# Two 64-row score products side by side, with sums and a root moved, in a two-block decoder kernel

## The chip, the cores and the metric

The kernel runs on one core of one Trainium2 chip. The metric is device time of one execution in microseconds (us), the median of the runs; lower is better. TensorE (PE) multiplies, VectorE (DVE), ScalarE (ACT) and GpSimd (POOL) do the rest, SyncE (SP) issues nearly all transfers.

## The reference

512 tokens of width 1024 in float32 pass through two decoder blocks. The change touches two parts of them. In the first block's first layer an indexer with 16 heads of 64 scores all keys; each token keeps its best 128 keys and attends to them:

```python
dots = jnp.einsum('bqhd,bsd->bqhs', qi, k_idx).astype(jnp.float32)
score = jnp.einsum('bqhs,bqh->bqs', jax.nn.relu(dots), wi.astype(jnp.float32))
score = jnp.where(causal[None], score, -jnp.inf)
_, idx = lax.top_k(score, topk)
```

Both layers of the first block also attend to a memory of 256 rows, with 4 heads of 64:

```python
s = jnp.einsum('bshd,bmhd->bhsm', q, k).astype(jnp.float32) * MEM_HEAD_DIM ** -0.5
p = jax.nn.softmax(s, axis=-1)
o = jnp.einsum('bhsm,bmhd->bshd', p, v.astype(jnp.float32)).astype(q_mem.dtype)
```

Everything else (projections, the attention to the chosen keys, gated feed-forward layers, a second block) stays as it is.

## The kernel before

All activations lie feature-major, 128 features by 512 tokens. Weights stream in as 334 chunks of eight 128x128 blocks. Of each chunk ScalarE makes a rounded high part (`split_hi`, into `w_hi`) and VectorE or GpSimd the rest (`split_lo`, into `w_lo`); each block is then three products of TensorE in one pass (high x high, high x low, low x high), 24 products a chunk, in `project`. `raw`, `w_hi` and `w_lo` have two halves, so a chunk can be loaded only when the chunk two before it has been split, and split only when that one has been used (`chunk_used`). `pj` (two PSUM banks) takes the projections; `take` on ScalarE copies one out.

Each engine runs one program written out by hand, in order; semaphores tie them. The stages of the first layer that matter here are:

- **Front** (to about 56 us): chunk 0 (index key), then 32 small products that sum squares (`sums("amix")`), chunk 1, in the middle of it `spread("amix")`, which turns the root of the mean square into a row factor; chunk 2 (first two index heads); a turn of the index weights; chunk 3 block by block with `sums("mem")`. VectorE needs the factor for the tables of the rotation (`tables_by_factor`, then `rope`), and splits chunk 3 after that.
- **Index** (to 130 us): eight tiles of two heads. A tile has six units, (head, token block) for blocks 1 to 3, of width 256, 384 and 512. `kidx` holds the keys twice: in one copy the features of the second head are zero, in the other those of the first, so that a product over all 128 rows gives one head. A unit is one plain float32 product into `ps[u % 2]` on TensorE, a relu into `s_sb[u % 2]` on ScalarE (which counts up `score_taken`), and a multiply-add into `score` on VectorE (`idx_added`). Between units TensorE projects the query of tile t+2, and ScalarE takes it after the relu of unit 4.
- **Selection** (to 212 us): VectorE finds 8 keys at a time for three token blocks, 16 rounds of six instructions (`rounds(n)`). Meanwhile TensorE projects the latent (`ckv`, 2 chunks), sums its squares, projects the memory keys and values (8 chunks of 256 columns, `mem_k`, `mem_v`; GpSimd splits these chunks) and the first queries. Between its rounds VectorE works off `means("ckv")`, waits for GpSimd's `inverse_root("ckv")`, and later does `apply("ckv")`: two products `hf`, ScalarE's rounding `norm_hi("ckv")` (`c_hi`, written after the last of the eight memory chunks in ScalarE's program), two differences `c_lo`.
- **Attention** `aq`, then `amem` over the memory. `amem` and, in the second layer, `bmem` run 2 tiles of 8 units (head, block). A unit passes from TensorE (`score_`) to VectorE (`maximum`, L1303 and L1314), ScalarE (`softmax`, L757), TensorE (`turn_p`, L2022), ScalarE (`bring`, L770) and TensorE (`values`, L2062). TensorE's program at unit u is: score of u + `ahead` (3), turn of u+1, values of u. `mem_k` holds keys with zero halves, as `kidx`.

## Time and profile before

| | us |
|---|---|
| median of 3 runs (lowest, highest) | 2417.23 (2413.25, 2422.09) |
| the profiled run's own time | 2415.6 |
| its span in the trace | 2413.8 |
| TensorE busy | 2273.4 (94%) |
| VectorE busy | 1298.2 (54%) |
| ScalarE busy | 921.1 (38%) |
| GpSimd busy | 250.7 (10%) |

The kernel is one long chain of stages, and TensorE is busy in nearly all of them, so what matters is which stretches are not set by it. The granted clock is TensorE's: 1.00 stands for 2.4 GHz and 0.50 for 1.2 GHz. A float32 product appears in the trace as two records, each with its own weight load; a product of rounded parts as one. The starts of neighbouring records give their true pace, since the ends are modelled and overlap.

### The profile page before, as it was taken

Reading aid. Unit: us, or ns where it says so; the run is one execution under the profiler, and the core shown is the slowest. Engines: PE = TensorE matmul, PEld = TensorE weight load, DVE = VectorE, ACT = ScalarE, POOL = GpSimd, SP = SyncE. Lnnn points to the kernel's source line nnn. Section 1 sums busy time; section 2 is a strip of 40 time slices with the busy share of each in tenths; the row PEclk is TensorE's granted clock in tenths of the full one; section 3 lists DMA queues with packets and bytes.
Section 4 is the critical chain, followed back from the end, with each engine's and each line's share of the span. In section 5 each row is a group of like instructions: output and inputs, shape, how many; then the busy total and the mean of one; then the engine's idle time right before and its main releaser. Section 6 shows DMA issues by size and latency. Waiting matters only on the chain.

```text
span 2413.8 us, 34422 instructions
## 1 busy us (share of the span) xinstructions
PE 2273.4 (94%) x10882; PEld 1855.7 (77%) x10882; DVE 1298.2 (54%) x2537; ACT 921.1 (38%) x1850; POOL 250.7 (10%) x143
## 2 busy tenths in 40 slices
PE   7986999999999799999999999999999689999997
PEld 6675777888888687788888888888887667777766
DVE  5876444666644566466664454555544643545443
ACT  4433453322322266432223332222223334555551
POOL 0042221000001111110000210000002000011112
PEclk8998999999999999999999999999999889999888
DMA  3121111332333110223232332222222312000001
GB/s 131 51 88 53 61 53 62 96 101 90 104 102 102 66 36 26 77 90 99 93 104 96 104 97 96 99 99 96 96 96 79 113 63 85 2 19 9 19 10 70
DMA packets 50053, 182.93 MB, mean 76 GB/s; under 512 B 5552, under 2 KB 5680, under 8 KB 49840
## 3 DMA queue, kind: packets, MB, share of 16 engines
q1 hardware_dynamic: 49824, 181.35, 22.9%
q8 instruction: 44, 0.72, 0.1%
q0 software_dynamic: 144, 0.52, 0.1%
q14 instruction: 41, 0.34, 0.0%
HBM read 179.76 MB, written 2.10 MB: 75 GB/s over the span
## 4 chain that ended last, share of the span: by engine, by line
PE 83%; DVE 7%; issue 4%; ACT 3%; POOL 1%; DMA 1%; DVEq 0%; ACTq 0%; POOLq 0%; SPq 0%
PE pj L1863 68%; PE ps L2006 4%; PE po L2062 4%; PE pt L2022 2%; ACT w_hi L670 1%; DMA raw<-in_wstream 1%; PE po L2047 1%; PE ps L2176 1%; DVE s_sb L1303 1%; PE pj L1973 1%; DVE rtmp L1248 1%; DVE w_lo L1118 1%; PE po L2071 1%; ACT p_sb L757 1%; DVE rtmp L1245 1%
## 5 line engine op out<-in xcount | busy, mean ns | idle before, releaser
L1863 PE MATMUL pj<-h_hi,w_hi 128*128 128x512 f32 x1736 | 706.9, 407 | 21.0 <-DVE w_lo L1118 15.6
L670 ACT ACTIVATE w_hi<-raw 128x1024 fp32r<-128x1024 f32 x334 | 353.7, 1059 | 865.6 <-PE pj L1863 848.8
L1863 PE MATMUL pj<-h_lo,w_hi 128*128 128x512 f32 x1736 | 683.8, 394 | 0.0
L1863 PE MATMUL pj<-h_hi,w_lo 128*128 128x512 f32 x1736 | 683.6, 394 | 0.0
L1118 DVE TENSOR_TENSOR w_lo<-raw,w_hi 128x1024 fp32r<-128x1024 f32 x288 | 390.4, 1356 | 392.2 <-ACT w_hi L670 391.9
L1863 PEld LDWEIGHTS pj<-h_hi,w_hi 128*128 128x128 f32 x1736 | 331.1, 191 | 90.1 <-issue 17.1
L1863 PEld LDWEIGHTS pj<-h_hi,w_lo 128*128 128x128 f32 x1736 | 330.5, 190 | 71.1
L1863 PEld LDWEIGHTS pj<-h_lo,w_hi 128*128 128x128 f32 x1736 | 331.5, 191 | 64.6 <-issue 1.4
L1863 PE MATMUL pj<-G_hi,w_hi 128*128 128x512 f32 x704 | 278.1, 395 | 3.1 <-DVE G_lo L1367 3.0
L1863 PE MATMUL pj<-G_lo,w_hi 128*128 128x512 f32 x704 | 276.0, 392 | 0.0
L1863 PE MATMUL pj<-G_hi,w_lo 128*128 128x512 f32 x704 | 275.9, 392 | 0.0
L1303 DVE CUSTOM_DVE_ANT_0 s_sb<-ps,cst 128x256 f32<-128x256 f32 (+4 forms) x264 | 102.1, 387 | 174.2 <-PE ps L2006 125.1
L757 ACT ACTIVATE p_sb<-s_sb,stats 128x256 f32<-128x256 f32 (+4 forms) x288 | 140.0, 486 | 125.1 <-DVE stats L1317 124.0
L579 POOL TENSOR_TENSOR w_lo<-raw,w_hi 128x1024 fp32r<-128x1024 f32 x46 | 109.8, 2387 | 545.6 <-ACT w_hi L670 545.6
L1863 PEld LDWEIGHTS pj<-G_hi,w_hi 128*128 128x128 f32 x704 | 133.6, 190 | 35.1 <-DVE G_lo L1367 3.8
L1863 PEld LDWEIGHTS pj<-G_hi,w_lo 128*128 128x128 f32 x704 | 133.4, 190 | 28.2
L2022 PE MATMUL pt<-cst,p_sb 128*128 128x128 f32 (+1 forms) x640 | 129.8, 285 | 26.7 <-ACT p_sb L757 25.8
L1863 PEld LDWEIGHTS pj<-G_lo,w_hi 128*128 128x128 f32 x704 | 133.6, 190 | 27.3
L2022 PEld LDWEIGHTS pt<-cst,p_sb 128*128 128x128 f32 (+1 forms) x640 | 86.3, 148 | 78.3 <-ACT p_sb L757 41.8
L770 ACT ACTIVATE pT<-pt 128x384 f32<-128x384 f32 (+3 forms) x320 | 119.2, 372 | 69.9 <-PE pt L2022 67.2
L553 POOL TENSOR_TENSOR ssum<-sq 128x512 f32<-128x512 f32 x6 | 9.4, 1563 | 981.1 <-ACT sq L837 981.1
L1170 DVE TENSOR_TENSOR fr<-pj,fac_f 128x512 f32<-128x512 f32 x44 | 30.4, 692 | 105.3 <-PE pj L1863 101.1
(295 smaller groups left out, 2531.4 us busy)
## 6 DMA issues: line engine op xcount, KB each, us to landing
raw<-in_wstream SPq DMA_DIRECT2D x334, 512.0 KB, 3.4
xT<-in_x SPq DMA_DIRECT2D x4, 512.0 KB, 9.5
out_x<-xT SPq DMA_DIRECT2D x4, 512.0 KB, 2.7
memT<-in_mem SPq DMA_DIRECT2D x1, 1024.0 KB, 12.3
cst<-in_cst SPq DMA_DIRECT2D x1, 512.0 KB, 10.5
tab<-in_tab POOLq DMA_DIRECT2D x1, 512.0 KB, 5.0
posi<-in_pos SPq DMA_DIRECT2D x1, 256.0 KB, 2.8
vec<-in_vec SPq DMA_DIRECT2D x1, 182.5 KB, 2.4
```

What stands on the lines that cost most here:

```text
L579: nc.gpsimd.tensor_tensor(w_lo[:, here], raw[:, here], w_hi[:, here].bitcast(f32), ALU.subtract).then_inc(lo_ready, 1)
L670: nc.scalar.activation(w_hi[:, c.par * CW:(c.par + 1) * CW], raw[:, c.par * CW:(c.par + 1) * CW], ACT.Copy).then_inc(hi_ready, 1)
L757: nc.scalar.activation(p_sb[:, par * S:par * S + w], s_sb[:, par * S:par * S + w], ACT.Exp, scale=rsm[:, b:b + 1] if branch == "mem" else ...
L770: nc.scalar.activation(pT[rows, par * S:par * S + n], pt[par][rows, 0:n], ACT.Copy).then_inc(pT_ready, 1)
L1118: nc.vector.tensor_tensor(w_lo[:, here], raw[:, here], w_hi[:, here].bitcast(f32), ALU.subtract).then_inc(lo_ready, 1)
L1170: nc.vector.tensor_tensor(dst, pj[t.par][:, 0:n], fac[name][:, 0:n], ALU.mult).then_inc(pj_free[t.par], 1)
L1245: link(nc.vector.stream_shuffle(rtmp[:, :], src, mask))
L1303: nc.vector.tensor_tensor_reduce(out=s_sb[:, par * S:par * S + w], in0=ps[par][:, 0:w], in1=bias(ph, u), scale=1.0, scalar=-3.0e38, op0=AL ...
L1863: mm = nc.tensor.matmul(acc, w[:, col:col + P], x[part], start=first and k == 0, stop=last and k == 2)
L2006: nc.tensor.matmul(ps[u % 2][:, 0:w], q[:, par * S + b * P:par * S + (b + 1) * P], keys, start=True, stop=True).then_inc(score_done, 1)
L2022: mm = nc.tensor.transpose(pt[par][0:wide, k * P:(k + 1) * P], p_sb[:, par * S + k * wide:par * S + (k + 1) * wide], ident)
L2062: mm = nc.tensor.matmul(acc, pT[:, par * S + k * P:par * S + (k + 1) * P], val, start=k == 0, stop=k == kbs - 1)
```

## The change

Keys are stored once, 64 rows for each head. The score of a head multiplies only its 64 rows, and the two heads of a block stand next to each other, so that the products use different halves of the array's rows. TensorE waits once for a pair, until both banks are free. `IDX_UNITS` and the memory units are ordered block by block; in `amem` and `bmem` TensorE issues the pair of u+2 and u+3 at each even u (`ahead` falls from 3 to 2). VectorE's add for the second head waits for the first head's. The blocks of the next index query follow each pair, three, three and two. In the front the squares are summed between the blocks of chunk 1, `spread("amix")` stands behind chunk 2, and the turn of the index weights behind chunk 3. In the selection `means("ckv")` follows 3 rounds instead of 6 and `apply("ckv")` 8 instead of 10, and GpSimd's root for it follows the third chunk instead of the sixth.

```diff
-        self.ahead = 3 if self.m == 8 else 2
+        self.paired = branches == ["mem"]
+        self.ahead = 3 if self.m == 8 and not self.paired else 2
...
-IDX_UNITS = [(hh, b) for hh in range(2) for b in range(1, NB)]
+IDX_UNITS = [(hh, b) for b in range(1, NB) for hh in range(2)]
...
+    beside = [(hh, b) for b in range(NB) for hh in range(2)]
...
-                if c == CH["mem"] + 5:
+                if c == CH["mem"] + 2:
                     inverse_root("ckv")
...
-            squares("amix", lambda m: (x_loaded[m // 2], 16))
             c, t = At(CH["afront"]), At(TL["afront"])
+            squares("amix", lambda m: (x_loaded[m // 2], 16), 0, 4)
             split_hi(c + 2)
             take(qn[:, 0:S], t, c)
+            squares("amix", lambda m: (x_loaded[m // 2], 16), 4)
             tables(0)
+            split_hi(c + 3)
             spread_factor("amix")
...
-            link(rope(ktmp[:, S:2 * S], qn[:, 0:S], tab_a, SHUF64, t))
-            for hh in range(2):
-                last = nc.vector.tensor_scalar(kidx[:, hh * S:(hh + 1) * S], ktmp[:, S:2 * S], V("half", hh), None,
-                                               ALU.mult)
-            last.then_inc(roped, 1)
+            rope(kidx[:, :], qn[:, 0:S], tab_a, SHUF64, t).then_inc(roped, 1)
...
-                    dve.wait_ge(idx_added, s + 1)
+                    dve.wait_ge(idx_added, s + 1 + hh)
...
-            rounds(6)
+            rounds(3)
             means("ckv")
             dve.wait_ge(rs_ready, STATS.index("ckv") + 1)
             nc.vector.tensor_tensor(rck[:, 0:NB], r4[:, 0:NB], rsa[:, 0:NB], ALU.mult).then_inc(rck_ready, 1)
+            rounds(5)
+            apply("ckv")
             rounds(4)
-            apply("ckv")
-            rounds(2)
...
-                pe.wait_ge(score_taken, ph.first_score + t * ph.n + u + 1)
-                nc.tensor.matmul(ps[u % 2][:, 0:w], q[:, par * S + b * P:par * S + (b + 1) * P], keys,
+                if not (ph.paired and hh):
+                    pe.wait_ge(score_taken, ph.first_score + t * ph.n + u + (2 if ph.paired else 1))
+                rows = slice(hh * 64, hh * 64 + 64) if branch == "mem" else slice(0, P)
+                nc.tensor.matmul(ps[u % 2][:, 0:w], q[rows, par * S + b * P:par * S + (b + 1) * P], keys[rows],
...
-                    score_(ph, i, j, u + ph.ahead)
+                    if not ph.paired:
+                        score_(ph, i, j, u + ph.ahead)
+                    elif u % 2 == 0:
+                        for e in range(2):
+                            score_(ph, i, j, u + 2 + e)
...
-            sums("amix")
-            pe.wait_ge(ld["cst"], 16)
-            for some in (range(4), range(4, CB)):
-                project(At(CH["afront"] + 1), At(TL["afront"] + 1), h_hi, h_lo, some=some)
-                if 0 in some:
-                    spread("amix")
+            for k in range(CB):
+                project(At(CH["afront"] + 1), At(TL["afront"] + 1), h_hi, h_lo, some=range(k, k + 1))
+                sums("amix", range(k, k + 1))
...
-                    if u < 4 and more:
-                        idx_query(i, j + 2, range(2 * u, 2 * u + 2))
+                    if hh and more:
+                        idx_query(i, j + 2, (range(0, 3), range(3, 6), range(6, CB))[u // 2])
             idx_query(0, 0)
-            turn(At(TL["afront"] + 1), TN["widx"])
+            pe.wait_ge(ld["cst"], 16)
+            spread("amix")
             for k in range(CB):
                 idx_query(0, 1, range(k, k + 1))
                 sums("mem", range(k, k + 1))
+            turn(At(TL["afront"] + 1), TN["widx"])
...
-                if k == 5:
+                if k == 4:
                     spread("ckv")
```

Left out above: `squares` and `take` get arguments for this, `mem_k` is written by one copy instead of two, the plain score of the index stage is cut into two 64-row halves in the same way, and the buffers shrink.

Three places show the order. The first is TensorE at the start of `amem`; `ps<-mem_k` is a score, `pt<-cst,p_sb` a turn (two products a unit), `po<-mem_v` the values (two a unit). Before:

```order
L2022 MATMUL pt<-cst,p_sb 128x128 [waits pT_ready,exp_done]
L2022 MATMUL pt<-cst,p_sb 128x128
L2062 MATMUL po<-mem_v_123,pT 128x64 [waits pT_ready,out_ready]
L2062 MATMUL po<-mem_v_123,pT 128x64
L2006 MATMUL ps<-mem_k_122,qn 128x256 [waits score_taken]
L2022 MATMUL pt<-cst,p_sb 128x128 [waits pT_ready,exp_done]
L2022 MATMUL pt<-cst,p_sb 128x128
L2062 MATMUL po<-mem_v_123,pT 128x64 [waits pT_ready]
```

And with the change, from the same turn (of unit 1) on, with its pair of scores ahead of it:

```order
L2002 MATMUL ps<-mem_k_122,qn 128x256 [waits score_taken]
L2002 MATMUL ps<-mem_k_122,qn 128x256
L2018 MATMUL pt<-cst,p_sb 128x128 [waits pT_ready,exp_done]
L2018 MATMUL pt<-cst,p_sb 128x128
L2058 MATMUL po<-mem_v_123,pT 128x64 [waits pT_ready,out_ready]
L2058 MATMUL po<-mem_v_123,pT 128x64
L2018 MATMUL pt<-cst,p_sb 128x128 [waits pT_ready,exp_done]
L2018 MATMUL pt<-cst,p_sb 128x128
L2058 MATMUL po<-mem_v_123,pT 128x64 [waits pT_ready]
L2058 MATMUL po<-mem_v_123,pT 128x64
L2002 MATMUL ps<-mem_k_122,qn 128x256 [waits score_taken]
L2002 MATMUL ps<-mem_k_122,qn 128x256
```

Before, a score stood ahead of every turn, of the unit two turns later; now two scores stand ahead of two turns, and the second of these turns is that of the first of the two scores.

The second place is TensorE at the end of an index tile (`pj<-h..` are products of the query of tile t+2, `ps<-kidx` scores). Before:

```order
L1863 MATMUL pj<-h_hi,w_hi 128x512
L1863 MATMUL pj<-h_lo,w_hi 128x512
L1863 MATMUL pj<-h_hi,w_lo 128x512
L2175 REGISTER_ALU
L2176 MATMUL ps<-kidx,qs 128x384 [waits score_taken]
L2175 REGISTER_ALU
L2176 MATMUL ps<-kidx,qs 128x512 [waits score_taken]
L2171 REGISTER_ALU
L2175 ISA [waits roped]
L2176 MATMUL ps<-kidx,qs 128x256 [waits score_taken]
```

With the change:

```order
L2175 MATMUL ps<-kidx,qs 128x512 [waits score_taken]
L2175 MATMUL ps<-kidx,qs 128x512
L1858 MATMUL pj<-h_hi,w_hi 128x512
L1858 MATMUL pj<-h_lo,w_hi 128x512
L1858 MATMUL pj<-h_hi,w_lo 128x512
L1858 MATMUL pj<-h_hi,w_hi 128x512
L1858 MATMUL pj<-h_lo,w_hi 128x512
L1858 MATMUL pj<-h_hi,w_lo 128x512
L2168 REGISTER_ALU
L2173 ISA [waits roped]
L2175 MATMUL ps<-kidx,qs 128x256 [waits score_taken]
L2175 MATMUL ps<-kidx,qs 128x256
```

The last two blocks of the query have moved behind the scores of units 4 and 5. The third place is ScalarE in the same tile, with the change; its order is that of before except for the widths (before: 384, the copy, 512, the split, 256):

```order
L937 ACTIVATE s_sb<-ps 128x512 [waits idx_added,score_done]
L926 REGISTER_ALU
L677 REGISTER_ALU [waits roped]
L678 ACTIVATE qn<-pj 128x512 [waits chunk_used]
L935 REGISTER_ALU
L937 ACTIVATE s_sb<-ps 128x512 [waits idx_added,score_done]
L670 ISA
L672 ACTIVATE w_hi<-raw 128x1024 [waits chunk_used,chunk_loaded0]
L935 ISA
L937 ACTIVATE s_sb<-ps 128x256 [waits idx_added,score_done]
```

The copy of the query (`qn<-pj`, which waits for the whole query) has stayed between the relus of units 4 and 5.

## Rows read from the trace of the kernel before

**Rows 1.** waits of TensorE: us in total, times, longest us

```profile
PE pt L2022 <- ACT p_sb L757: 25.8, 18, 16.1
```

**Rows 2.** timeline, VectorE, selection: start us, us, instruction [idle before <-releaser]

```profile
133.77 1.48 DVE L1620 MAX8 m<-score 128x8 f32<-128x256 f32 x3 [0.20 <-DVE score L1613]
...
167.34 0.16 DVE L1631 TENSOR_TENSOR rck<-r,rsa 128x4 f32<-128x4 f32 x1 [8.90 <-POOL r L567]
...
182.09 1.41 DVE L1227 SCALAR_TENSOR_TENSOR hf<-ckv,vec,po 128x512 f32<-128x512 f32 x2 [0.21 <-DVE score L1624]
...
185.95 1.48 DVE L1620 MAX8 m<-score 128x8 f32<-128x256 f32 x3 [0.27 <-DVE c_lo L1213]
```

**Rows 3.** timeline, same stage, on TensorE, GpSimd and ScalarE

```profile
146.25 0.99 PE L1907 MATMUL po<-ones,sq 128*128 128x1 f32 x4
...
152.93 2.40 POOL L579 TENSOR_TENSOR w_lo<-raw,w_hi 128x1024 fp32r<-128x1024 f32 x1 [7.88 <-ACT w_hi L670]
...
165.67 1.64 POOL L567 TENSOR_TENSOR r<-v,mhalf 128x8 f32<-128x8 f32 x1
...
183.21 0.63 ACT L979 ACTIVATE mem_v<-pt,rv 128x128 f32<-128x128 f32 x2 [4.91 <-PE pt L1949]
183.72 1.15 ACT L710 ACTIVATE c_hi<-hf 128x512 fp32r<-128x512 f32 x2
```

**Rows 4.** timeline, bmem attention: TensorE (4), VectorE (1), ScalarE (2)

```profile
964.07 0.44 PE L2022 MATMUL pt<-cst,p_sb 128*128 128x128 f32 x2 [0.28 <-ACT p_sb L757]
...
967.75 0.65 PE L2006 MATMUL ps<-mem_k,qn 128*128 128x256 f32 x2
...
968.24 0.38 PE L2022 MATMUL pt<-cst,p_sb 128*128 128x128 f32 x2
...
968.85 0.65 PE L2006 MATMUL ps<-mem_k,qn 128*128 128x256 f32 x2
...
968.62 0.42 DVE L1303 CUSTOM_DVE_ANT_0 s_sb<-ps,fac_mem 128x256 f32<-128x256 f32 x1 [0.42 <-PE ps L2006]
...
963.32 0.60 ACT L757 ACTIVATE p_sb<-s_sb,stats,rsm 128x256 f32<-128x256 f32 x1 [0.40 <-DVE stats L1314]
...
969.34 0.60 ACT L757 ACTIVATE p_sb<-s_sb,stats,rsm 128x256 f32<-128x256 f32 x1
```

**Rows 5.** timeline, index stage: TensorE (2), ScalarE (2)

```profile
66.10 0.58 PE L1863 MATMUL pj<-h_hi,w_hi 128*128 128x512 f32 x1
...
75.52 0.58 PE L1863 MATMUL pj<-h_hi,w_hi 128*128 128x512 f32 x1
...
65.59 0.59 ACT L676 ACTIVATE qn<-pj 128x512 f32<-128x512 f32 x1
...
66.55 1.06 ACT L670 ACTIVATE w_hi<-raw 128x1024 fp32r<-128x1024 f32 x1
```

**Rows 6.** chain in order of time (start us, us, what); timeline of ScalarE

```profile
130.56 10.91 PE pj L1863 x48
...
141.56 1.06 ACT L670 ACTIVATE w_hi<-raw 128x1024 fp32r<-128x1024 f32 x1 [3.89 <-PE pj L1863]
```

**Rows 7.** TensorE by shape: 32-row and 128-row products: xcount | busy, mean ns

```profile
L2047 PE MATMUL po<-cmp_v,pT 32*128 x64 | 15.0, 317 | 0.0
...
L2062 PE MATMUL po<-n_vs,pT 128*128 x160 | 21.7, 267 | 0.0
```

**Rows 8.** timeline of the front: TensorE, then VectorE

```profile
35.39 0.60 PE L1930 MATMUL po<-cst,r 128*128 128x128 f32 x4
...
46.30 0.38 PE L1907 MATMUL pt<-ones,sq 128*128 128x1 f32 x2 [0.98 <-ACT sq L685]
...
42.31 1.22 DVE L1118 TENSOR_TENSOR w_lo<-raw,w_hi 128x1024 fp32r<-128x1024 f32 x1
```

**Rows 9.** busy us by stretch (PE PEld DVE ACT POOL), granted clock, DMA

```profile
27.50:31.00 3.50, 3.50 (x18) 3.50 (x18) 1.23 (x1) 3.10 (x5) 0.00 (x0) 0.50 0.02 5
...
122.70:130.20 7.50, 6.75 (x15) 2.98 (x16) 5.93 (x12) 3.23 (x7) 0.00 (x0) 0.77 0.00 0
```

More of the change, by code:

```diff
@@ L676, in take, with squares @@
                 nc.scalar.activation(dst, pj[t.par][rows, 0:n], func, scale=scale).then_inc(pj_free[t.par], 1)
-            def squares(name, waits):
+            def squares(name, waits, start=0, stop=None):
                 src, n, _, _, _, _ = NORM[name]
-                for m in range(dict(NORMS)[name]):
+                for m in range(start, stop or dict(NORMS)[name]):
                     sem_, value = waits(m)
@@ L941, in _ @@
             idx_query(0, 0)
+            squares("mem", lambda m: (ld["mem"], 16))
             act.wait_ge(v_turned, TN["widx"] + 1)
@@ L944, in _ @@
                                  ACT.Copy, scale=1024.0 ** -0.5)
[L945 removed]
+            split_hi(At(CH["idx"] + 3))
             tables(1)
[L947 removed]
             idx_query(0, 1)
@@ L968, in _ @@
                     if k < 2:
-                        act.wait_ge(chunk_used, c.v + 3)
-                        for hh in range(2):
-                            last = nc.scalar.activation(mem_k[l][:, (2 * k + hh) * MEM:(2 * k + hh + 1) * MEM],
-                                                        pj[t.par][:, 0:MEM], ACT.Copy, scale=V("half", hh))
-                        last.then_inc(pj_free[t.par], 1)
+                        take(mem_k[l][:, k * MEM:(k + 1) * MEM], t, c, n=MEM)
                     else:
@@ L1995, in score_ @@
                 elif branch == "mem":
-                    k_at = (2 * t + hh) * MEM
-                    keys = mem_k[0 if ph.name == "amem" else 1][:, k_at:k_at + MEM]
+                    keys = mem_k[0 if ph.name == "amem" else 1][:, t * MEM:(t + 1) * MEM]
                 elif branch == "band":
```

22 lines of the change are left out of this document (10 added, 12 removed).

## The prediction

> **What bounds the kernel now.** I read the chain of work that ended last and TensorE's list of waits first. TensorE is busy for 94% of the span, so a stretch of the change is worth something only where TensorE sets its end, and the question of each stretch is what ends last there. TensorE's longest single wait, 16.1 us, is at the start of the attention `aq` [rows 1]: all of the selection stage is set by VectorE's 16 rounds, not by TensorE. The timeline of that stage shows VectorE's two waits, 8.90 us for GpSimd's root and the time from `hf` to the end of `c_lo` [rows 2], and what held the root and ScalarE's `c_hi` back [rows 3]. The timeline of `bmem` shows a ring of three engines, in which a unit's score, maximum, exponential, turn and values follow each other [rows 4]. In the index stage TensorE is the bound, with 9.42 us a tile [rows 5].
>
> **Selection, +7.3 us.** Four rounds fill 167.5 to 182.1 us, 3.65 us each [rows 2]. Before, `apply("ckv")` begins at 182.09, after 10 rounds, and ends at 185.7. Its second half needs `c_hi`, and ScalarE writes `c_hi` at 183.72, right behind the last `mem_v`, for which it had waited 4.91 us on TensorE [rows 3]: that time is TensorE's, which works through ckv, eight memory chunks and the first query. Nothing in the change shortens that list. With the change VectorE does 3 rounds to 144.7 us (10.9 us from 133.77). It then waits for the sums of squares, which end at 147.2 [rows 3]. The root follows GpSimd's third split, which ends at 155.3, and takes 1.64: 157.0, where before it came at 167.3. Five rounds end at 175.4, the two `hf` at 176.8, and there VectorE waits 7 us for the same `c_hi` at 183.7. `apply` ends at 185.7 as before, but with 8 rounds behind it instead of 10: two rounds more to do, 2 x 3.65 = 7.3 us. The earlier root earns nothing, since the wait has moved to `c_hi`. TensorE's 16.1 us wait grows by as much, so all of it is on the path. Bounds: 5.6 if TensorE's list ends 1.7 us sooner, because the root no longer stands between two later splits; 8.9 if the root, now ahead of the fourth split, delays it by its 1.64.
>
> **Memory attention, +11 us for both.** The steps of the ring from start to start are: score to maximum 0.87, maximum to exponential 0.72 (967.75, 968.62, 969.34), exponential to turn 0.75 (963.32, 964.07), turn through values to next score 0.61 (968.24, 968.85) [rows 4]. Before, a score stood two turns ahead of its own turn, and a unit came each 1.10 us (967.75, 968.85). With the change a pair of scores is followed by two turns, the second of which belongs to the first score of the pair; the next pair stands behind it. So one pair needs a whole ring: 0.87 + 0.72 + 0.75 + 0.61 = 2.95, with ScalarE's copy between turn and values 3.0 us, where two units took 2.2. That is +0.8 for each of the five full rounds of the ring in a stage of eight pairs (the ends of the stage balance): +4.0 a stage. What the narrower products save on TensorE is hidden here, since TensorE waits. On top comes the clock: with 1.3 us of products in 3.0 instead of in 2.2 TensorE is less busy, and where scores alone ran, at 122.7 to 130.2 us, the granted clock was 0.77 on the mean, a part of it at the level of 0.50 [rows 9]. At that level the product and the turn cost about 1.0 more in a ring. I take 1.5 a stage; the ends are 0 and 5. Sum (4.0 + 1.5) x 2 = 11, from 2 (if half of the ring is covered by something that I don't see) to 18.
>
> **Index stage, +5 us.** Of 9.42 us a tile [rows 5] the 24 products of a query take 24 x 0.227 = 5.45 (48 in 10.91 [rows 6]), so the six scores cost 3.97. Side by side they cost between 1.98 (the two heads fully together) and 3.97 (not at all). Each float32 product is two records in a row; of the four records of a pair only the second of the first head and the first of the second can lie side by side if records run in program order, as all timelines show them. I take three quarters, 2.98. The trace has no change between full and part-height products except the 32-row values of the compressed branch: 317 ns a record against 267 for 128 rows [rows 7]; 0.05 on four records gives 0.2 a pair, and 0 is the other end. I take 0.15, so 0.45 a tile. Then a new wait: the query's last two blocks now follow the scores of units 4 and 5, while ScalarE's copy of the query still stands between these two relus. TensorE ends the blocks, ScalarE starts 0.26 later (last product's pace end at 141.30, ScalarE at 141.56 [rows 6]), copy and relu take 0.96 (65.59 to 66.55 [rows 5]), the release 0.1: 1.3 us, in which TensorE waits for `score_taken` ahead of the next tile's pair. Queued behind it are that pair and all of the next query. Tile: 5.45 + 2.98 + 0.45 + 1.3 = 10.2, against 9.42: 6 x 0.8 = +4.7. VectorE (some 7.7 us a tile with its rotation, split and adds) fits inside, except in tiles 1 and 2, where the rotation of the latent key and a table come on top; the second head's relu now waits behind more of VectorE's list: +1.5. The last two tiles, without a query, gain 1. Together +5.2. The ends of the two unknown prices give tiles of 8.7 and 11.3: -4 and +12.
>
> A rule speaks for more. The Trainium skill, TensorEngine Tiling (Array Packing), Theoretical Speedup, gives up to 2 times where the contraction is 64 or less; with it and no other cost a tile would be 5.45 + 1.98 + 1.3 = 8.7. The same page, Key Properties, says that changing the tiling mode drains TensorE, which speaks against the change, as here it changes twice a pair. No row shows two products side by side.
>
> **Front, +1.5 us.** Eighteen records of the sums took 3.5 us at a granted clock of 0.50 [rows 9]; between dense blocks they should keep the full level, and with the blocks that followed at half speed this saves about 5 us. But the spread, at 35.39 before, now also stands behind four more blocks of chunk 1 and the eight of chunk 2, 12 x 0.68 = 8.2 us: 35.4 + 8.2 - 5 = 38.6. From the spread to the low part of chunk 3 VectorE needed 43.53 - 35.39 = 8.1 [rows 8], now 7.3 without the two products for the zero halves. Chunk 3 is ready at 45.9, and TensorE waits 7 us for it. Before, TensorE did its first block by 45.3, when a wait of 1.0 for the memory squares began [rows 8], so it had begun some 0.9 earlier, at 44.4: chunk 3 starts 1.5 later, and the wait of 1.0 is saved. The turn of the index weights now comes last, and ScalarE's split, tables and copy behind it; that costs another 1. Bounds: -1 if the interleaved sums cost half, +5 if the clock stays at the lower level.
>
> The smaller edits (one copy of `mem_k` for two, smaller buffers) lie on ScalarE beside longer waits: 0, and 0.4 each if they were not.
>
> **Sum.** 7.3 + 11 + 5.2 + 1.5 = +25.0 us. The profiled run took 2415.6, which gives 2440.6; it was 1.6 below the median of the runs, 2417.2, from which it would be 2442. I take 2441, 1.0% slower.
>
> **Rivals.**
> (A) As above, 2441.
> (B) The heads lie fully together and the change of height costs nothing: a tile of 8.7, index stage -4.3 + 0.5 = -3.8, memory 9, selection 7.3, front 1.5: +14, 2430. For it: different rows, different banks. Against it: the order of the records.
> (C) Nothing overlaps and the lower clock is frequent: tile 11.3, index +11, memory 14, selection 8, front 4: +37, 2453.
> (D) The change doesn't do what it moves: the ring of `amem` and the copy in the index tile are covered, because ScalarE and VectorE answer sooner to pairs, and only the selection's two rounds are left against small gains in front: +7, 2423.
> (E) Faster. TensorE alone sets the index stage: tile 5.45 + 1.98 = 7.43, 2 us less, -12 in all; in front -5; memory -1 each; the selection still +7.3. That is -12, 2404. It decides from the point where ScalarE's copy of the query no longer ends behind TensorE's own work, and the ring takes under 2.2 us a pair. Against it: both orders are fixed in the programs.
>
> **Chances.** A 0.45, B 0.24, C 0.13, D 0.10, E 0.08. The range takes in B, A and most of C and cuts D: 2422 to 2456. Faster by over 0.3% (7 us; about what a measurement of this kernel can tell from no change): 0.09, E and a little of D. Within: 0.07, half of D and the low end of B. Slower: 0.84.
>
> **What would show it.** In the selection: VectorE waits about 9 us for the root after 3 rounds and about 7 us ahead of `c_lo`, and TensorE's wait for the exponential in `aq` is some 23 us. In `bmem`: pairs of scores 3.0 us apart, with TensorE waiting for `p_sb` once a pair. In the index stage: TensorE waits over 1 us for a relu at each tile's start, tiles of about 10.2 us, and the second head's first record starts with the first head's second. In front: TensorE idle for some 7 us ahead of chunk 3. Wrong would be: `c_hi` well before 183 us (measured from the end of the index scores, 53 us behind it), a ring under 2.4 us, or tiles under 8.5 us.

## The result, and the profile after

Measured side by side, the changed kernel takes 2466.81 us (median of 4 runs, 2464.62 to 2467.02) and the kernel before 2416.69 (4 runs): a ratio of 1.0203 with a 95% interval of 1.0183 to 1.0223, so 2.0% slower. The forecast was 2441, 1.0% slower, with 2422 to 2456 as its range: the sign was right, the size about half, and the result lies above the range. The profiled executions have spans of 2413.8 and 2462.8 us, 49.0 apart. To see where they go, the start of the same TensorE record or VectorE instruction is read in both traces, at the seams of the stages:

| seam | before | after | later by | stage between |
|---|---|---|---|---|
| first product | 12.95 | 12.03 | -0.9 | |
| first index score | 56.34 | 62.89 | +6.5 | front, +7.5 |
| first MAX8 | 133.77 | 149.54 | +15.8 | index scores, +9.2 |
| `bias_a` | 211.56 | 233.54 | +22.0 | selection, +6.2 |
| first score of `amem` | 344.4 | 366.7 | +22.3 | attention `aq`, +0.3 |
| first output product behind `amem` | 371.4 | 406.6 | +35.2 | `amem`, +12.9 |
| first score of `bmem` | 961.1 | 997.0 | +35.9 | between, +0.6 |
| first output product behind `bmem` | 986.2 | 1036.0 | +49.8 | `bmem`, +13.9 |

What stands behind is 0.8 us shorter than before. The page's slices (a digit is the share of full speed that the throttle granted, in tenths, over 61.6 us) show where the clock is lower than before: in the third and fourth slice (123 to 246 us, 8 and 7 for 9 and 8), in the seventh, where `amem` is (6 for 9), in the seventeenth, where `bmem` is (6 for 9), and, behind the change, in the thirty-fifth (8 for 9):

```profile
PEclk8987996999999999699999999999999889899888
```

**Front.** The windows of TensorE (stretch in us, its length, busy time and number of records, granted clock) show one stretch without work and what follows it:

```profile
core 0: us, PE busy (x), PEclk, DMA share, GB/s
24.00:38.00 14.00, 14.00 (x85) 1.00 0.11 39
38.00:44.70 6.70, 0.13 (x2) 0.88 0.01 2
44.80:61.90 17.10, 17.10 (x57) 0.50 0.20 61
62.90:66.80 3.90, 3.90 (x12) 0.50 0.06 13
68.00:93.00 25.00, 20.38 (x85) 1.00 0.14 49
```

The sums between the blocks of chunk 1 ran at the full level, as forecast. TensorE then waits 6.6 us for the low part of chunk 3 and resumes at 44.8 (before: 44.4, without that wait [rows 8]). But with full work from then on its clock stays at 0.50, the level of 1.2 GHz, for 22 us: a step of three products and two pairs of sums takes 2.13 us, eight of them 17.

**Index scores.** From TensorE's and ScalarE's timelines of a middle tile:

```profile
114.00 0.49 ACT L937 ACTIVATE s_sb<-ps 128x384 f32<-128x384 f32 x1 [2.39 <-PE ps L2175]
114.98 0.49 ACT L937 ACTIVATE s_sb<-ps 128x384 f32<-128x384 f32 x1 [0.49 <-DVE score L1583]
...
116.17 1.13 PE L2175 MATMUL ps<-kidx,qs 64*128 64x512 f32 x4
117.33 0.60 ACT L937 ACTIVATE s_sb<-ps 128x512 f32<-128x512 f32 x1 [1.86 <-PE ps L2175]
118.92 0.60 ACT L678 ACTIVATE qn<-pj 128x512 f32<-128x512 f32 x1 [0.99 <-PE pj L1858]
119.42 0.59 ACT L937 ACTIVATE s_sb<-ps 128x512 f32<-128x512 f32 x1
120.06 0.70 PE L2175 MATMUL ps<-kidx,qs 64*128 64x256 f32 x4 [1.18 <-ACT s_sb L937]
```

The wait that the forecast had put there is in the last row: ScalarE's copy (L678) stands between the two relus of 512 columns, and TensorE waits 1.18 us ahead of the next tile's first pair. The pair itself is another matter. Asked for the line of the scores in the first half microsecond of the 512-column pair, the trace gives two products of 693 ns whose first and last start are the same tenth:

```profile
L2175 PE MATMUL ps<-kidx,qs x2: 693/693/693, 116.2 to 116.2; 64*128 64x512 f32 x2
```

and the timeline shut behind that half microsecond holds two records of 0.69 in 0.70 us:

```profile
116.17 0.70 PE L2175 MATMUL ps<-kidx,qs 64*128 64x512 f32 x2
```

These are the first records of the two heads, not the two records of one: the two that report a finished score (one for each head) start together as well, 0.53 us later (116.71). The heads run fully side by side, and a pair costs as much as one head. What it pays beside that lies at the change of height, in and out: from the last product in front to the second product behind (less their own 0.23 each, and less the wait) the pairs of 256, 384 and 512 columns take 0.84, 1.05 and 1.26 us. One full-height head took 0.43, 0.65 and 0.87 before, so each pair costs 0.40 us on top. The six scores of a tile thus cost 3.15 us against 3.9.

Tile by tile (start of the first score of a tile to that of the next, the last one to MAX8), before: 9.51, 9.42, 12.47, 9.80, 9.53, 9.42, 8.42, 8.85. After: 11.81, 9.93, 14.96, 10.58, 9.89, 10.00, 8.59, 10.89. The sum is 9.2 more: 2.3 in the first tile, which runs at the clock that the front left; 2.5 in the third, where VectorE's list is longest; 2.0 in the last, at a granted clock of 0.50 from 131.9 us on; and some 0.5 in each of the others.

**Selection.** VectorE's timeline:

```profile
162.49 0.22 DVE L1136 TENSOR_SCALAR vg<-ps 128x1 f32<-128x1 f32 x2 [2.25 <-PE po L1902]
...
172.17 2.33 DVE L1626 TENSOR_TENSOR rck<-r,rsa 128x4 f32<-128x4 f32 x1 [8.92 <-POOL r L569]
...
192.67 1.41 DVE L1226 SCALAR_TENSOR_TENSOR hf<-ckv,vec,po 128x512 f32<-128x512 f32 x2 [0.21 <-DVE score L1619]
199.63 1.29 DVE L1212 TENSOR_TENSOR c_lo<-hf,c_hi 128x512 fp32r<-128x512 f32 x2 [5.55 <-ACT c_hi L712]
```

The wait for the root has not shrunk (8.92 where it was 8.90 [rows 2]), it only begins three rounds sooner; and a new wait of 5.55 us for `c_hi` stands ahead of `c_lo`. From MAX8 to `bias_a` it is 84.0 us where it was 77.8. TensorE's two waits at the start of `aq`, before:

```profile
196.03 1.62 PE L2006 MATMUL ps<-a_k,qs 128*128 128x128 f32 x4 [2.64 <-issue]
213.76 0.48 PE L2022 MATMUL pt<-cst,p_sb 128*128 128x128 f32 x1 [16.11 <-ACT p_sb L757]
```

and with the change:

```profile
218.65 1.62 PE L2002 MATMUL ps<-a_k,qs 128*128 128x128 f32 x4 [10.01 <-issue]
235.74 0.47 PE L2018 MATMUL pt<-cst,p_sb 128*128 128x128 f32 x1 [15.47 <-ACT p_sb L759]
```

The wait for the exponential has not grown; the one ahead of the first score has, by 7.4 us. VectorE's rotation of the query, which this score reads, ends 0.1 us ahead of it in both kernels (195.93 and 218.55), and stands behind all the rounds but the last four.

**Memory attention.** Two pairs of `bmem` on TensorE:

```profile
1004.72 1.23 PE L2002 MATMUL ps<-mem_k,qn 64*128 64x256 f32 x4
1005.88 0.69 PE L2018 MATMUL pt<-cst,p_sb 128*128 128x128 f32 x2
1006.36 0.95 PE L2058 MATMUL po<-mem_v,pT 128*128 128x64 f32 x4
1007.62 0.69 PE L2018 MATMUL pt<-cst,p_sb 128*128 128x128 f32 x2 [0.31 <-ACT p_sb L759]
1008.10 0.95 PE L2058 MATMUL po<-mem_v,pT 128*128 128x64 f32 x4
1008.99 1.23 PE L2002 MATMUL ps<-mem_k,qn 64*128 64x256 f32 x4
```

and the window over five of them:

```profile
1003.00:1024.00 21.00, 19.43 (x81) 0.50 0.21 71
```

Pairs are 4.27 us apart, not the 3.0 of the forecast and not the 2.2 of before [rows 4]. TensorE waits only 0.31 us in each: it is busy for 93% of the stretch, but at 1.2 GHz throughout. That is the largest part of what the forecast missed, and the first question for the experiments.

### The profile page after: what moved, and what is told of

Read it like the earlier page. It is cut to its first block, busy times and chain, and to the rows that moved or that the text cites. A ratio compares the mean times of both kernels' runs of the same rounds, so it can differ in the third digit from the quotient of the medians.

```text
span 2462.8 us, 34399 instructions
## 1 busy us (share of the span) xinstructions
PE 2292.8 (93%) x10882; PEld 1860.4 (76%) x10882; DVE 1297.5 (53%) x2535; ACT 918.5 (37%) x1846; POOL 250.0 (10%) x143
## 4 chain that ended last, share of the span: by engine, by line
PE 84%; DVE 6%; issue 4%; ACT 3%; POOL 1%; DMA 1%; DVEq 0%; ACTq 0%; POOLq 0%; SPq 0%
PE pj L1858 68%; PE ps L2002 5%; PE po L2058 4%; PE pt L2018 3%; ACT w_hi L672 1%; PE po L2043 1%; PE ps L2175 1%; DMA raw<-in_wstream 1%; PE pj L1968 1%; DVE s_sb L1302 1%; DVE w_lo L1117 1%; PE po L2067 1%; DVE rtmp L1247 1%; ACT p_sb L759 1%; DVE rtmp L1244 1%
## 5 line engine op out<-in xcount | busy, mean ns | idle before, releaser
L2018 PE MATMUL pt<-cst,p_sb 128*128 128x128 f32 (+1 forms) x640 | 137.6, 299 | 35.0 <-ACT p_sb L759 34.3
```

What stands on the lines that cost most here:

```text
L2018: mm = nc.tensor.transpose(pt[par][0:wide, k * P:(k + 1) * P], p_sb[:, par * S + k * wide:par * S + (k + 1) * wide], ident)
```

## The experiments

Each kernel is the one before with the edit named, unless the text says otherwise. "Ratio" is against the kernel before, measured beside it. With the order of its products unchanged the front has, from one profile to the next, a stretch at 0.50 behind some 46 us that is 0 to 17 us long, and the first index score stands 41 to 48 us behind the first product. The first product itself starts at 10.7 to 13.1 us, and what stands behind `bmem` is 0.8 us shorter to 4.9 longer than before, though no kernel changes anything there. So stages are compared from their own first record, and whole kernels by medians.

**The four parts alone.** The change falls into four sets of edits that touch nothing of each other. First, the memory attention, with `beside` for the units of `amem` and `bmem`:

```diff
+    beside = [(hh, b) for b in range(NB) for hh in range(2)]
-                    score_(ph, i, j, u + ph.ahead)
+                    if not ph.paired:
+                        score_(ph, i, j, u + ph.ahead)
+                    elif u % 2 == 0:
+                        for e in range(2):
+                            score_(ph, i, j, u + 2 + e)
...
+                rows = slice(hh * 64, hh * 64 + 64) if branch == "mem" else slice(0, P)
```

> The kernel before with only the memory attention changed (64-row products of two heads as pairs, pairs of scores two units ahead). Theory M: the trace after shows 13.4 us lost in amem and 14.2 in bmem (TensorE's start of the same record against before: +22.2 ahead of amem, +35.6 behind it, +49.8 behind bmem), with pairs 4.26 us apart at a granted clock of 0.50; these are of the memory attention alone, so this kernel is +27 us (range 24 to 30), 2444. Rival R: part of the loss comes from the other edits (the root, the first part's clock); then the pairs here are some 3.0 us apart at the full level and the kernel is +8 to +12 us, 2427.

2446.8 us, +27.5, ratio 1.0100 (1.0081 to 1.0119). Its `amem` is 13.6 us longer and its `bmem` 13.9, with the clock at 0.50 from 351 to 392 and from 979 to 1007 us. The whole loss belongs to this part, whatever stands ahead of it.

The selection (3, 5 and 4 rounds for 6, 4 and 2, `inverse_root` behind `CH["mem"] + 2`, `spread("ckv")` at k == 4):

> The kernel before with only the selection changed (3, 5 and 4 rounds, root behind GpSimd's third memory split, spread one chunk sooner). Theory: c_hi is set by TensorE's list, so two rounds more stand behind apply: +6.2 to +7.3 us, 2423.5. Rival: the order of rounds costs nothing by itself and the 6.2 us that the trace after shows in this stage come from the later and slower index stage ahead of it: within 1 us of before.

2423.73 us, +4.4, ratio 1.0020 (1.0004 to 1.0037): less than the 6.2 to 7.3 expected, though its interval holds them. From MAX8 to `bias_a` it is 5.8 us longer, so the loss of this stage comes from its own edits and not from what stands ahead of it. The rounds, the root and the spread were not run apart; that the rounds are what costs is read from VectorE's waits.

The first part (`sums("amix", range(k, k + 1))` behind each block of chunk 1, `spread("amix")` behind `idx_query(0, 0)`, squares and splits as in the change):

> The kernel before with only the first part changed (sums of squares between the blocks of chunk 1, spread behind the first index query, ScalarE's and VectorE's splits and squares moved). Theory F: the trace after has the granted clock at 0.50 from 43.2 to 67.0 us, behind a TensorE idle of 6.7 us, where before had 48.0 to 51.4; the first index score starts 7.5 us later relative to the first product, and 1.9 us more go into the first index tile at that level: +9 us, 2426. Rival: the lower level over that stretch comes from the 64-row products or is chance; then the clock here is as before and the kernel is +1.5 us, 2418.5.

2425.1 us, +5.8, ratio 1.0024 (1.0013 to 1.0034). Its trace repeats the changed kernel's: TensorE waits 7.6 us for chunk 3, and then

```profile
44.80:62.00 17.20, 15.87 (x51) 0.50 0.19 61
```

with the clock at 0.50 from 43.6 to 67.4. Up to MAX8 the profile is 9.7 us longer than before, counted from the first product.

The index scores (units in pairs, `kidx` without zero halves, `rows`, blocks 3, 3 and 2 behind the pairs):

> The kernel before with only the index scores changed (64-row products in pairs, blocks 3, 3 and 2 behind the pairs). Theory I: tiles of 9.90 us in the middle (three pairs of 0.84, 1.05 and 1.26, the query's 5.45, and 1.25 of waiting for ScalarE's second relu behind the copy) against 9.42, 1.9 more where VectorE's list is longest, and the last two tiles: +6 to +8 us, 2424. Rival: the 9.2 us of the trace after are for the greater part the lower clock of the first tile, which the first part's order brings; then +2 to +4 us, 2420.

2422.01 us, +2.7, ratio 1.0016 (1.0004 to 1.0028). Tiles are 9.93, 9.93, 15.58, 10.58, 9.91, 10.00, 8.58 and 10.89: the middle and the last as in the changed kernel, the first without its 1.9 at the lower level, so that tile's loss came from the front. The third costs 3.1 more than before. Counted in its own profile from the first product to MAX8 this is +7.1, the number of theory I (+8.0 from the first score on, with a front 0.9 shorter); the median is that of the rival, though the first tile's clock, on which the rival rested, is worth only 1.9.

The four differences of medians add up to 40.5, the four stage accounts (27.5, 5.8, 9.7 and 7.1) to 50.1, against 50 for the whole. By the stages the parts simply add. The medians of the first part and of the index scores come out some 4 us each lower. For the first part that is the kernel before: its profiled run took 2415.6 us, where its median beside these four is 2419.3, and all eight runs of front_alone lie at 2424 to 2429. The span of index_alone is only 2.7 us longer than before in the profiles too: its first product starts 2.3 us earlier, and its stages behind MAX8 are 2.1 us shorter. Why they are, no run shows.

**What slows the memory ring?** The same order of scores as in mem_alone, but full-height products and keys with zero halves (the line with `rows` taken out again):

> The kernel before with the order of the memory scores alone changed (two scores in a row, two units ahead), but with full-height products and keys with zero halves. Theory O: the order makes the ring, and with it the waits behind which TensorE's granted clock stays at 0.50, so pairs are some 4.2 us apart as with the 64-row products and the kernel is +25 us (range 20 to 30), 2443. Rival S: the switch between full and 64-row products is what slows the ring; then pairs are 3.0 us apart at the full level and the kernel is +8 us, 2426.

2428.94 us, +12.0, ratio 1.0052 (1.0035 to 1.0068). That lies between the two numbers, nearer to rival S. Its `amem` and `bmem` are 4.7 and 5.0 us longer than before, and pairs of scores stand 3.10 us apart:

```profile
977.12 1.08 PE L2009 MATMUL ps<-mem_k,qn 128*128 128x256 f32 x4
...
980.22 1.08 PE L2009 MATMUL ps<-mem_k,qn 128*128 128x256 f32 x4
```

Over this ring the clock is at the full level, although TensorE waits far more than in the changed kernel:

```profile
974.00:990.00 16.00, 12.92 (x86) 1.00 0.21 66
```

That is the ring of the forecast, 2.95 to 3.0, at nearly the price of the forecast, 4.0 a stage. So waiting is not what took the clock down; the other 15 us of mem_alone (by the two profiles 9.0 in `amem` and 8.9 in `bmem`) come with the 64-row products.

The reverse, 64-row products one at a time in the old order (the old `ahead`, the old `pair`, the line with `rows`, each key stored once):

> The kernel before with 64-row products in the memory attention, but one at a time in the old order of units and three ahead. In the index stage a pair of 64-row products took 0.41 us more than its 0.43 for two concurrent ones of 256 columns; here nothing runs beside a score, so each of the 32 scores takes 0.84 instead of 0.43, and TensorE sets this ring (100% busy in the rows of before): 32 x 0.41 = +13 us, 2432. Rival: the 0.41 belongs to the pair and not to the change of height; then 0, 2419. A third: the wait lowers the clock too, then +20.

2451.53 us, +34.6, ratio 1.0150 (1.0124 to 1.0177): worse than all three numbers. A score starts every 2.51 us, and the window says why:

```profile
980.00:1010.00 30.00, 30.00 (x96) 0.50 0.15 50
```

TensorE works without a pause and its clock stays at 0.50, from 344 to 389 and from 976 to 1023 us. A single 64-row score of 256 columns holds TensorE for 1.15 us at that level, as long as a pair does.

Then the pairs with as many scores under way as before:

```diff
-                    elif u % 2 == 0:
+                    elif u % 2:
                         for e in range(2):
-                            score_(ph, i, j, u + 2 + e)
+                            score_(ph, i, j, u + 3 + e)
```

> 64-row products in pairs as in the change, but the pair stands ahead of the turn of the second unit behind it (three and four units ahead), so as many scores are under way as before. Theory O: the order made the ring; here TensorE finds both banks free, a pair takes 0.84 + 0.4 + 0.9 = 2.2 us at the full level as two units did before, and the kernel is within 3 us of before, 2419. Rival S (the switch itself makes the ring slow and the clock low): +15 us or more.

2433.93 us, +17.0, ratio 1.0070 (1.0047 to 1.0093). The waits are gone, as theory O said, but the clock is not back:

```profile
970.00:990.00 20.00, 20.00 (x88) 0.50 0.21 80
```

A pair now takes 3.69 us, all of it TensorE's own work at 1.2 GHz. And the same with full-height products, so that only the height of the scores differs (and with it the keys with zero halves, which ScalarE writes in two copies instead of one):

> mem_ahead3 with full-height products and keys with zero halves, nothing else changed. Theory H (height): the 64-row products bring the level of 0.50; here the clock is as before, a pair takes 2.2 us, and the kernel is within 3 us of before, 2418. Rival P (pairs): the pairing three ahead itself costs the 17 us of mem_ahead3; then it is near 2434 here too.

2420.23 us, +3.5, ratio 1.0012 (1.0000 to 1.0023), a little over the 3 us of theory H and far from the 2434 of rival P; `amem` and `bmem` are 1.9 and 0.4 us longer than before, and

```profile
966.00:980.00 14.00, 14.00 (x99) 1.00 0.33 107
```

with 2.27 us a pair. Both kernels keep TensorE busy for 100% of the ring. With 128-row scores it is granted the full level, with 64-row scores the lower one. Theory H holds.

The traces say more closely what the height does. The clock also falls with full-height scores: in all sixteen profiles, that of the kernel before included, it goes to 0.50 some 3 to 4 us behind the first score of `amem`, where TensorE still waits for the first units to come round. Before, in windows from 347.5 us on (busy us of PE, PEld, DVE, ACT and POOL, then the granted clock):

```profile
347.50:351.00 3.50, 3.22 (x13) 2.53 (x14) 1.98 (x10) 2.90 (x9) 0.77 (x1) 0.63 0.37 116
351.00:354.00 3.00, 3.00 (x19) 2.52 (x19) 1.29 (x6) 1.84 (x6) 0.00 (x0) 0.86 0.10 40
354.00:358.00 4.00, 4.00 (x32) 3.69 (x31) 2.26 (x10) 3.58 (x12) 0.00 (x0) 1.00 0.00 0
```

In the eleven kernels with full-height scores in `amem` it is back after 3 to 7 us; in the four with 64-row scores and nothing added it stays down for 27 to 44 us. In `bmem` it does not fall within the stage with full-height scores, and falls 1.6 to 2.2 us behind the first score with 64-row ones. So with 64-row scores the clock falls where it otherwise holds, and does not come back where it otherwise does.

Last, useless full-height work in the ring of mem_ahead3:

```diff
+                if ph.paired:
+                    pe.wait_ge(pT_ready, a + 1)
+                    nc.tensor.matmul(pt[par][:, 256:512], ident, cst[:, 0:256], start=True, stop=True)
                 pe.wait_ge(exp_done, a + 3)
```

> mem_ahead3 with one useless full-height float32 product of 256 columns ahead of each turn (two a pair, 0.86 us at the full level). Theory: the level follows how much of TensorE's time is full-height work; with more of it the clock is at the full level for much of the stage, and a pair takes 2.2 + 0.86 = 3.1 us against 3.69 without the extra work: 16 x 0.6 = 9 us faster than mem_ahead3, 2424. Rival: the level stays at 0.50 while 64-row products run; then a pair takes 3.69 + 1.7 = 5.4 us and the kernel is 27 us slower than mem_ahead3, 2461.

2436.85 us, +20.1, ratio 1.0087 (1.0064 to 1.0109). By its time the theory failed: it is not 9 us faster than mem_ahead3 but about equal. Its trace shows that the clock does rise. In `amem` it is at 0.50 only from 351.4 to 354.9, and in `bmem` it rises after a start at 0.50 and stays:

```profile
983.00:1000.00 17.00, 17.00 (x117) 1.00 0.18 63
```

and from then on a pair takes 2.97 us (983.23, 986.20) with its extra 0.9 us of products, against 3.69 without them. But a stage has only eight pairs, four in each of its two tiles, and both the start of `bmem`, at 0.50 from 972.7 to 982.9, and the extra work are paid for; in sum its two memory stages are 14 us longer than before, where those of mem_ahead3 are 19: 5 of the 9 us expected. The rest of its profile's 23 us is a front of the slower kind (5.6 up to MAX8) and, on balance, 3.6 in stages that the edit does not touch. So the lower level is not fixed once 64-row products run.

**What slows the front?** front_alone with seven float32 products in TensorE's wait:

```diff
             spread("amix")
+            for k in range(7):
+                nc.tensor.matmul(ps[0][:, :], ident, cst[:, 0:S], start=True, stop=True)
```

> The first part changed as in front_alone, plus seven useless float32 products of 512 columns on a free bank in TensorE's wait of 6.7 us ahead of chunk 3 (some 6 us at the full level); nothing else is changed. Theory: the wait is what the lower level of the clock follows; with it filled the blocks behind it run at the full level, the loop of blocks and sums takes some 12 us instead of 17, and the kernel is 5 to 8 us faster than front_alone, 2418. Rival: the one-column sums between the blocks bring the lower level; then the clock is 0.50 from 44 to 67 us as before and the time is that of front_alone or up to 1 us more, 2425.

2420.58 us, ratio 1.0013 (0.9997 to 1.0029). front_alone had 1.0024 (1.0013 to 1.0034), so by the timed runs it is some 3 us faster, with intervals that overlap, and the 5 to 8 expected are not shown. Its ten runs fall into two groups, five at 2413 to 2418 us and five at 2423 to 2426; the profiled one is of the first, while all eight of front_alone are at 2424 to 2429. Up to MAX8 the two profiles are 10 us apart, and in span 6.3. The windows that answer to those of the changed kernel:

```profile
38.00:44.70 6.70, 6.70 (x22) 1.00 0.01 2
44.80:56.50 11.70, 10.14 (x62) 1.00 0.27 91
```

A step takes 1.14 us instead of 2.13, and there is no stretch at 0.50 before 143 us. So the one-column sums do not bring the lower level by themselves, and in this profile it did not come once the wait was filled (1.6 us of it are left). What the filler did in the five longer runs no profile shows.

Two things in the other profiles limit this. Thirteen kernels have the old front, with a wait of only 1.0 us ahead of the sums; in eight the clock holds, in the kernel before it is at 0.50 for 3 us, and in the other four (mem_alone, mem_ahead3_fill, and index_copy_last and best, which come below) for 14 to 17. So a long wait is not needed. And in six of the seven profiles with a low stretch here, the changed kernel and front_alone among them, the clock comes back only 2 to 6 us behind the last of the one-column sums. Once the level is low, the sums may be what holds it there; no run takes them out of the loop, so that stays open.

**Is there a gain in the index pairs?** ScalarE's copy of the query moved from `u == 4` to `u == 5`, behind both relus:

> index_alone with ScalarE's copy of the query moved behind the second head's last relu (unit 5 instead of 4). Theory: the 1.25 us per tile that TensorE waits ahead of the 256-column pair is the copy; without it a tile is 5.45 + 0.84 + 1.05 + 1.26 = 8.6 us against 9.90 in index_alone and 9.42 before, over six tiles -7.5 us against index_alone and -5 against before, 2412 to 2414. Rival: ScalarE's relus or VectorE's sums are the bound of the pair order anyway; then the wait stays over 0.8 us and the kernel is that of index_alone, 2420.

2417.46 us, ratio 0.9992 (0.9977 to 1.0006), where index_alone had 1.0016: level with before, some 5 us under index_alone by the ratios, and short of the 2412 to 2414 expected. The middle tiles are 8.78 and 8.88 us, close to the 8.6 expected, so the wait was the copy. But the stage does not keep it: the third tile is 15.06 (12.47 before), and the last two, at 0.50 from 125.6 to 139.2 us, 9.31 and 10.89 (8.42 and 8.85). From its first score to MAX8 this profile is 5.7 us longer than before, of which some 1.6 is a first tile at the lower clock of a slow front.

The same with full-height products:

> The same order and copy as index_copy_last, but full-height products with keys with zero halves: what is left of the difference is the 64-row products alone. Theory: a full-height product costs 0.43, 0.65 and 0.87 us by width, six of them 3.9 a tile against 3.15 for the three pairs, so this is 0.75 x 6 = 4.5 us slower than index_copy_last, about as before, 2417. Rival: the switch of height and the clock eat the gain; then both are equal.

2423.26 us, ratio 1.0025 (1.0010 to 1.0041), 5.8 above index_copy_last, where 4.5 was expected. Its middle tiles are 9.42 and its third is 16.47, with

```profile
83.28 2.93 PE L2177 MATMUL ps<-kidx,qs 128*128 128x512 f32 x3 [3.87 <-ACT s_sb L934]
```

So in the middle tiles the 64-row products do earn their keep, 0.6 us a tile. Over the whole stage the two profiles are nearly equal (83.1 us in index_copy_last, 83.3 here), because the last two tiles give it back, 20.2 us against 18.1. TensorE's windows over them, first index_copy_last, then this kernel:

```profile
126.00:139.00 13.00, 8.46 (x21) 0.50 0.09 36
120.00:137.00 17.00, 11.54 (x38) 1.00 0.10 31
```

That is the effect of the memory stages in a second place: in the last two index tiles the clock is at 0.50 for 14 to 17 us in all four kernels with 64-row index scores, and for 0 to 3 in the twelve others.

It is the order in pairs that loses: with full-height products and the copy moved, the stage is 5.8 us longer than before. A pair needs both score banks free at once, and in the tile with VectorE's extra work both relus queue behind it (the row above).

**A version that beats both.** The wait for the root in the selection is filled, not moved:

```diff
             rounds(6)
             means("ckv")
+            rounds(2)
             dve.wait_ge(rs_ready, STATS.index("ckv") + 1)
...
             apply("ckv")
-            rounds(2)
```

> The kernel before with one edit: of the rounds behind apply two are moved between the sums for the root and the wait for it, so 12 instead of 10 stand ahead of apply. Theory: VectorE's wait of 8.90 us for the root is filled with two rounds of 3.65, while c_hi comes no sooner than TensorE's list lets it (183.7 us); -7.3 us, 2410. Rival: the root or c_hi move back by as much, or TensorE's first attention has another bound; then 0.

2409.79 us, 7.0 less than before, ratio 0.9977 (0.9961 to 0.9994). From MAX8 to `bias_a` it is 70.3 us instead of 77.8. VectorE's waits fall to 1.91 for the root and 0.77 for `c_hi`, and at the start of `aq` TensorE waits 4 us less [rows 1]:

```profile
201.97 0.48 PE L2022 MATMUL pt<-cst,p_sb 128*128 128x128 f32 x1 [12.26 <-ACT p_sb L757]
```

> index_copy_last and select_8 together, the memory attention and the first part as before. Theory: -5 and -7.3 add up, some 12 us faster than before, 2405 (ratio 0.995). Rival: the earlier end of the index stage leaves TensorE's list as the bound of c_hi and so of apply; then 8 us.

2410.51 us, ratio 0.9980 (0.9964 to 0.9996). That is short of both 12 and 8 us. The two do not add up, because index_copy_last had no gain to add (in this profile the index stage is 5.2 us longer than before and the selection 6.5 shorter); select_8 by itself is the better kernel, since it is as fast with one edit.

## Why the prediction was half right

**Selection, forecast +7.3, measured +6.2 (5.8 alone).** VectorE's steps hold one by one: VectorE waits for the sums (2.25), for the root (8.92; some 9 forecast), and ahead of `c_lo` (5.55; 7 forecast). Of the 1.1 us between forecast and measurement 0.5 is `c_hi`, which ScalarE begins 49.4 us behind the first MAX8 instead of 50.0 (183.72 [rows 3]), as the lower bound of 5.6 had allowed for; 0.6 lies in the last four rounds, which take 15.1 us where the same four took 15.7. TensorE's wait for the exponential in `aq` was to grow from 16.1 to 23 us and did not (15.47). The forecast had left out that the query's rotation stands on VectorE behind the moved rounds: the time went into TensorE's wait ahead of its first score (10.01 where it was 2.64). The stage is longer all the same, since VectorE's last round ends it.

**Memory attention, forecast +11, measured +26.8.** The failed step is the term for the clock, 1.5 us a stage with an end of 5. The ring itself was right: 3.0 us a pair and 4.0 a stage were forecast, mem_order_full has 3.10, and 4.7 and 5.0 a stage. The forecast had the clock fall because TensorE would be *less busy*. That reason is false here, as three kernels show: at 81% busy with full-height scores the level is 1.00, at 93 and at 100% with 64-row scores it is 0.50. In place of 1.5 the 64-row products cost 9 us a stage. (The sum's lower bound, 2, is also mis-added: half of 4.0 in each of two stages is 4.) The forecast had even named a stretch at 0.50 where scores ran almost alone [rows 9], but took it as a matter of density and not of what kind of product runs. The bound of 18 was too low for the same reason; rival C, which held "the lower clock is frequent", came closest and gave it 14.

**Index stage, forecast +5.2, measured +9.2.** The tile was 10.2 and is 9.9. Behind this near hit two errors cancel in part. The step "only two of the four records can lie side by side" is wrong: the heads' first records start together, and the heads take the time of one, as rival B had it. The price of changing the height, taken as 0.15 us a pair from a row of another kind of product [rows 7], is 0.40. The Trainium skill, TensorEngine Tiling (Array Packing), Key Properties, has both halves of this: tiles work independently, and a change of mode drains the engine. The trace agrees with the first, which is worth one head's time, up to 0.87 a pair. It shows 0.40 a pair beside it, which may be the drain; no run takes that 0.40 apart. At 256 columns the two cancel to 0.03. The wait for the copy was forecast at 1.3 and is 1.2. What made 9.2 of 5.2 lies outside the middle tiles: 1.9 of the first tile belongs to the front's clock, the third tile lost 2.5 where 1.5 was set for VectorE's extra, and the last two tiles, forecast at -1, lost 2.2, again at the level of 0.50 while 64-row scores ran without blocks between them.

**Front, forecast +1.5, measured +7.5.** The wait of 7 us for chunk 3 was forecast and came (6.6), and so did the full level under the sums between the blocks of chunk 1. The failed step is the term "starts 1.5 later", which ends its account where TensorE resumes. What the clock may do behind the wait was kept only as the outer bound, +5. The eight steps alone took 17.0 us where front_warm's, at the full level, would take 9.1: 8 us. The one profile of front_warm shows the link to the wait; whether the sums of `mem` held the level down is open.

**Small edits** were forecast at 0; nothing in the traces says otherwise.

Of the signs named in advance, VectorE's two waits in the selection, the index tile's wait and the front's idle time came as stated; TensorE's wait for the exponential did not. The sign for `bmem`, pairs 3.0 us apart, was missed (4.27), and so was that of the records in order (the second head starts with the first's first record). One thing, a clock at half speed, makes 18 us in the memory attention (3 were forecast), 8 in the front and some 4 in the first and last index tiles: 27 us more than forecast, where 25 were missed, and that the other misses nearly cancel is luck.

## What to carry to other kernels

Two half-height products side by side cost the time of one plus 0.40 us at the change of height, so in this kernel they pay from 384 columns up and not at 256; and where they fill a stage with little full-height work between them, look for a clock at half level before counting on a gain. When a change opens a wait on TensorE, price what follows it too: 6.6 us without work were followed by 22 us at half speed, and in four profiles 1.0 us by 14 to 17. And a wait on one engine can be filled with work that has to be done anyway: two of the 16 rounds in VectorE's wait gave 7 us, where moving the wait lost 6.

## What the runs showed of the hardware

- The first float32 records of two heads on rows 0 to 63 and 64 to 127, into two banks, start together: two records of 693 ns in 0.70 us. A 64-row score alone takes as long as the pair (1.15 us for 256 columns at 0.50).
- A pair at the full level: 0.84, 1.05 and 1.26 us for 256, 384 and 512 columns, against 0.87, 1.30 and 1.74 for two full-height scores.
- Granted clock of the memory ring: 1.00 with full-height scores, at 81% and at 100% busy; 0.50 with 64-row scores, at 93% and at 100% busy; 1.00 again in most of `amem` and the later part of `bmem` with two more full-height products of 256 columns in each pair. Why the chip grants less with 64-row products, no run here can tell.
- At the start of `amem` the clock falls to 0.50 in all sixteen profiles; it is back after 3 to 7 us with full-height scores, and after 3 with 64-row scores among added full-height products; with 64-row scores alone it stays down for 27 to 44.
- Behind a wait of 7.6 us (front_alone) and of 6.6 (the changed kernel) the front ran at 0.50 for 21 and 22 us of steady work; in the one profile with seven useless products in that wait it stayed at 1.00.
